# Where GpSimd's splits stand between VectorE's combinations, and which operand VectorE's spread sums read

## The reference, cut to what matters

```python
# group A: 4 heads, differential; two softmaxes per head, one subtracted from the other
p = probs(qb1, k1) - lam * probs(qb2, k2)
ao = einsum('bhqk,bkhd->bqhd', p, v)          # then rmsnorm per head, times silu(ag)
# group B: 8 heads of width 64; each row attends to its 256 best keys by an indexer score
s  = einsum('bqhd,bqkhd->bhqk', qb, kg) * scale + bias
bo = einsum('bhqk,bqkhd->bqhd', softmax(s), vg)   # times silu(bg)
y  = rmsnorm(x + einsum('bse,ed->bsd', concatenate([ao, bo]), w_out))
```

## Time and profile before

| | |
|---|---|
| median of three runs | 738.67 us |
| profiled execution | 737.92 us |
| span of the profile | 736.1 us |
| TensorE busy | 714.5 us (97%) |
| VectorE busy | 615.0 us (84%) |
| GpSimd busy | 363.1 us (49%) |
| ScalarE busy | 321.6 us (44%) |

### The profile page before, as it was taken

The page is one execution under the profiler, slowest core; times in us unless marked ns, Lnnn a source line. Parts: engine busy times, 40 slices in busy tenths (PEclk is TensorE's granted clock), DMA queues, the critical chain, the costliest instruction groups (busy, mean ns, idle before and its releaser), DMA issues.

```text
span 736.1 us, 12004 instructions
## 1 busy us (share of the span) xinstructions
PE 714.5 (97%) x4112; PEld 592.7 (81%) x4112; DVE 615.0 (84%) x1351; ACT 321.6 (44%) x723; POOL 363.1 (49%) x445
## 2 busy tenths in 40 slices
PE   8999999999999899999999999999999999999996
PEld 7757888888888788888888888888787878788886
DVE  5578999999998889888699999999789888546554
ACT  7547131131313666666631131314877767522222
POOL 5220222223556769771135654546999999612210
PEclk9999999999999999999999999999999999999999
DMA  7351211211220010213021112130010122313231
GB/s 282 108 145 46 52 49 44 57 44 46 66 76 1 0 44 1 51 31 101 16 71 45 43 44 57 44 87 0 30 45 11 50 55 91 116 58 100 73 115 57
DMA packets 25140, 45.10 MB, mean 61 GB/s; under 512 B 3140, under 2 KB 11512, under 8 KB 24952
## 3 DMA queue, kind: packets, MB, share of 16 engines
q1 hardware_dynamic: 23912, 43.28, 20.2%
q10 hardware_dynamic: 1168, 1.05, 0.4%
HBM read 35.92 MB, written 6.57 MB: 58 GB/s over the span
## 4 chain that ended last, share of the span: by engine, by line
PE 51%; DVE 23%; POOL 18%; issue 4%; ACT 2%; DMA 2%; POOLq 0%; SPq 0%; ACTq 0%; DVEq 0%
PE psum L1288 24%; PE psum L1509 12%; DVE score L1655 10%; DVE top L1650 10%; POOL k_high_twice L628 3%; PE psum L1383 2%; PE psum L1371 2%; PE psum L1208 2%; PE psum L1180 2%; POOL qT_r L631 2%; POOL k_zero_low L631 2%; POOL q_low_high L631 2%; POOL kT_r L631 2%; POOL near_low L769 2%; PE psum L1349 2%
## 5 line engine op out<-in xcount | busy, mean ns | idle before, releaser
L624 POOL TENSOR_TENSOR w_lo<-w_raw,w_hi 128x512 fp32r<-128x512 f32 x60 | 77.5, 1294 | 214.7 <-ACT w_hi L822 214.4
L1655 DVE MATCH_REPLACE8 score<-top,score 128x640 f32<-128x640 f32 (+5 forms) x176 | 157.4, 908 | 0.0
L1650 DVE MAX8 top<-score 128x8 f32<-128x640 f32 (+5 forms) x176 | 148.7, 911 | 1.2
L822 ACT ACTIVATE w_hi<-w_raw 128x512 fp32r<-128x512 f32 x60 | 37.4, 629 | 209.8 <-PE psum L1288 206.8
L998 ACT ACTIVATE probs<-psum,small 128x384 f32<-128x384 f32 (+7 forms) x128 | 94.6, 740 | 39.5 <-DVE small L1748 38.0
L1288 PE MATMUL psum<-big_hi,w_hi 128*128 128x512 f32 x256 | 99.7, 389 | 0.0
L1288 PE MATMUL psum<-big_hi,w_lo 128*128 128x512 f32 x256 | 99.6, 389 | 0.0
L1288 PE MATMUL psum<-big_lo,w_hi 128*128 128x512 f32 x256 | 99.6, 389 | 0.0
L1288 PE MATMUL psum<-w_hi,big_hi 128*128 128x512 f32 x192 | 74.7, 389 | 0.0
L1288 PE MATMUL psum<-w_lo,big_hi 128*128 128x512 f32 x192 | 74.7, 389 | 0.0
L1288 PE MATMUL psum<-w_hi,big_lo 128*128 128x512 f32 x192 | 74.7, 389 | 0.0
(11 more groups left out here) (199 smaller groups left out, 1608.8 us busy)
## 6 DMA issues: line engine op xcount, KB each, us to landing
w_raw<-in_w_in SPq DMA_DIRECT2D x62, 256.0 KB, 2.7
xs<-in_x SPq DMA_DIRECT2D x8, 512.0 KB, 6.5
k_high_twice<-k_high_twice SPq DMA_DIRECT2D x16, 256.0 KB, 3.7
xres<-in_x SPq DMA_DIRECT2D x8, 512.0 KB, 4.8
out_y<-y_out SPq DMA_DIRECT2D x8, 384.0 KB, 2.9
w_tail<-in_w_out SPq DMA_DIRECT2D x10, 256.0 KB, 2.6
bias_scratch<-bias_row SPq DMA_DIRECT2D x1, 2304.0 KB
bias<-bias_scratch SPq DMA_DIRECT2D x12, 128.0 KB, 3.1
```

The lines of the kernel that those rows point to most:

```text
L624: pool.tensor_tensor(lo[:, 0:cols], w_staged(n)[:, 0:cols], hi[:, 0:cols].bitcast(f32), ALU.subtract).then_inc(w_lo_made, 1)
L822: act.activation(w_parts(n)[0][:, 0:cols], w_staged(n)[:, 0:cols], ACT.Copy).then_inc(w_hi_made, 1)
L1650: ins = dve.max(top8[:, i - SEL0, :], sc)
L1655: ins = dve.match_replace(sc, top8[:, i - SEL0, :], sc, TAKEN)
```

## The change

In the first attention a quarter split is cut in two (`steps`): part 0 has the first three instructions, part 1 the last two with the signal. Each part has a step of its own, and waits, beside the gate of its step, for `combined` to reach s + 3, which is the combination of step s + 2. Block 1's quarters 2 and 3 go to the steps 0 to 3, block 2's four quarters to the steps 4 to 11, block 3's to the steps 12 to 19. In the second attention `share` becomes a product of a constant tile of ones, which lies in PSUM in the second 128 columns of `BACK_BANK`, with the two inverted sums; a memset before the loop fills the ones.

```diff
-            def split_k(ph, b, half):
+            def split_k(ph, b, half, steps=(0, 1)):
...
-                link(rounded(k0[0:HEAD, c], kT[0:HEAD, b, c]))
-                link(rounded(k1[HEAD:P, c], kT[HEAD:P, b, c]))
-                link(rest(k1_low[b % 2][HEAD:P, c], kT[HEAD:P, b, c], k1[HEAD:P, c]))
-                link(rest(kT_r[0:HEAD, b, c], kT[0:HEAD, b, c], k0[0:HEAD, c]))
-                ins = pool.memset(kT_r[HEAD:P, b, c].bitcast(f32), 0.0)
-                if half == 1:
-                    ins.then_inc(kh_made, 1)
...
+                if 0 in steps:
+                    link(rounded(k0[0:HEAD, c], kT[0:HEAD, b, c]))
+                    link(rounded(k1[HEAD:P, c], kT[HEAD:P, b, c]))
+                    link(rest(k1_low[b % 2][HEAD:P, c], kT[HEAD:P, b, c], k1[HEAD:P, c]))
+                if 1 in steps:
+                    link(rest(kT_r[0:HEAD, b, c], kT[0:HEAD, b, c], k0[0:HEAD, c]))
+                    ins = pool.memset(kT_r[HEAD:P, b, c].bitcast(f32), 0.0)
+                    if half == 1:
+                        ins.then_inc(kh_made, 1)
...
-                ahead = s + 3
-                if s < 2 or ahead >= TILES and ahead % TILES < 4 and ahead < 3 * TILES:
+                ahead = s + 4
+                if s < 4 or ahead >= TILES and ahead < 3 * TILES:
                     pool.wait_ge(o_gated, s + 1)
-                if s < 2:
-                    split_part(0, 1, s + 2)
-                elif ahead >= TILES and ahead % TILES < 4 and ahead < 3 * TILES:
-                    split_part(0, ahead // TILES + 1, ahead % TILES)
+                    pool.wait_ge(combined, s + 3)
+                if s < 4:
+                    split_part(0, 1, 2 + s // 2, (s % 2,))
+                elif ahead >= TILES and ahead < 3 * TILES:
+                    split_part(0, ahead // TILES + 1, ahead % TILES // 2, (ahead % 2,))
...
+            ones = bank(BACK_BANK)[:, P:2 * P]
...
-                dve.tensor_copy(shares[:, :, :], rinv[:, c:c + 2].unsqueeze(2).broadcast_to([P, 2, HEAD])
-                                ).then_inc(shares_made, 1)
+                dve.tensor_tensor(shares[:, :, :], ones.rearrange("p (m d) -> p m d", m=2),
+                                  rinv[:, c:c + 2].unsqueeze(2).broadcast_to([P, 2, HEAD]), ALU.mult
+                                  ).then_inc(shares_made, 1)
...
             dve.wait_ge(bank_moved, moved[9])
+            link(dve.memset(ones, 1.0))
```

More of the change, by code:

```diff
@@ L631, in rest, with split_q @@
                 return pool.tensor_tensor(out, src, high.bitcast(f32), ALU.subtract)
-            def split_q(ph, b, half):
+            def split_q(ph, b, half, steps=(0, 1)):
                 c = slice(half * HALF, (half + 1) * HALF)
@@ L649, in split_k @@
-            def split_k(ph, b, half):
+                if 0 in steps:
+                    link(rounded(q1[HEAD:P, c], qT[HEAD:P, b, c]))
+                    link(rest(q1[0:HEAD, c], qT[HEAD:P, b, c], q1[HEAD:P, c]))
+                    link(rounded(part, qT[0:HEAD, b, c]))
+                if 1 in steps:
+                    link(rest(qT_r[HEAD:P, b, c], qT[0:HEAD, b, c], part))
+                    ins = rounded(qT_r[0:HEAD, b, c], qT[0:HEAD, b, c])
+                    if half == 1:
+                        ins.then_inc(split, 1)
+                        pool.wait_ge(split, ph * BLOCKS + b + 1)
+                    else:
+                        link(ins)
@@ L658, in split_k @@
-                if half == 1:
-                    ins.then_inc(kh_made, 1)
[L660 to L664, removed]
+                if 0 in steps:
+                    link(rounded(k0[0:HEAD, c], kT[0:HEAD, b, c]))
+                    link(rounded(k1[HEAD:P, c], kT[HEAD:P, b, c]))
+                    link(rest(k1_low[b % 2][HEAD:P, c], kT[HEAD:P, b, c], k1[HEAD:P, c]))
+                if 1 in steps:
+                    link(rest(kT_r[0:HEAD, b, c], kT[0:HEAD, b, c], k0[0:HEAD, c]))
+                    ins = pool.memset(kT_r[HEAD:P, b, c].bitcast(f32), 0.0)
+                    if half == 1:
+                        ins.then_inc(kh_made, 1)
+                        pool.wait_ge(kh_made, ph * BLOCKS + b + 1)
+                    else:
+                        link(ins)
@@ L666, in split_part @@
+            def split_part(ph, b, j, steps=(0, 1)):
                 if j == 0 and b == 1:
                     wait_chunk_used(pool, (A_GROUPS, B_GROUPS)[ph][-1] * DB + DB - 1)
-                elif j == 0:
+                elif j == 0 and 0 in steps:
                     pool.wait_ge(s_ready, units_before(ph, b - 1))
-                (split_q, split_q, split_k, split_k)[j](ph, b, j % 2)
+                (split_q, split_q, split_k, split_k)[j](ph, b, j % 2, steps)
             def project_low(ph):
```

## The result

The changed kernel took 752.25 us in the median of four runs, against 738.32 us for four runs of the kernel before: the ratio is 1.0179, with a 95% interval of 1.0159 to 1.0200. The direction was as forecast, but the loss is 13.9 us instead of 4.6. The profiled execution has a span of 751.3 us, 15.2 more than before.

A forecast was written before the change was run, and what follows sets the result against it. The prediction took TensorE, busy 97% of the span, to bound the kernel. Added waits of 9.7 us less gains of 4.8 and 0.3 us made it 4.6 us slower, 743.3 us, range 740.2 to 747.0.

The forecast's parts named there:

- TensorE waits for the key copies at three block ends: First attention, starts of blocks 1 to 3: later key copies make TensorE wait 2.8, 4.1 and 2.8 us.
- The second wait is the longest, because of the low part in step 10: Block 2's start: the low part awaits ScalarE's high part, delaying the key's last difference; TensorE waits 4.1 us.
- What the first attention gains: First attention, splits moved behind combinations: less GpSimd contention with VectorE saves 4.8 us, bounds 3.0 and 6.1 us.
- Most of the contention goes: First attention: split parts fit the gaps between combinations; block 1's eight combinations fall from 9.9 to 7.5 us or less.
- The shares: Second attention: shares take 0.28 to 0.3 us each; only the last block gains, 0.3 us, bounds nothing and 0.9.
- The sum of the added waits as their price: First attention: three added TensorE waits cost their summed length, 9.7 us, bounds 8.6 and 11.5 us.
- every new wait of TensorE is paid in full: Whole kernel: TensorE is busy 97% of the span, so each added wait lengthens the time by its own length.
- The keys were not in time: Rival, block ends: copy and memset fit into TensorE's remaining work, only gains stay, 733.6 us; chance 0.07.
- gains and waits did not cancel: Rival, whole kernel: full gains of 6.1 and 0.9 us offset the waits, 738.8 us; chance 0.12.
- the pile-up after a wait: First attention, after each wait: VectorE and ScalarE start the next block with nothing behind them, giving back 0.5 us each.
- GpSimd did not fall behind: Rival, first attention: GpSimd's lateness piles up, gain 2 us, waits 12.7 us, time 749.1 us; chance 0.16.
- The forecast of a slower kernel: Whole kernel: the change makes it slower, by 4.6 us in the main forecast; chance of slower 0.78.

The follow-up runs named there:

- the kernel with early copies: Changed kernel with key copies signalled by the second rounding they read, not the later difference and memset: 734.43 us, ratio 0.9932 to the kernel before.
- its first part alone: Changed kernel with shares made by the copy again, only the first attention's splits changed: 751.23 us, ratio 1.0166 to the kernel before.
- the long waits: Kernel before, only the first attention's key copies for blocks 1 to 3 held until the combination of the block's seventh step: 756.93 us, ratio 1.0251.

## Why the prediction was wrong, step by step

- **TensorE waits for the key copies at three block ends: right.** Forecast 2.8, 4.1 and 2.8 us, 9.7 in all; measured 3.13, 4.10 and 3.33 us, 10.6 in all. The path was the forecast one: difference, memset, two issues, a copy of 3.96 us (3.86 us in the second case), 0.25 us to the start. The two shorter ones were a little longer because the combination of the sixth step, 1.03 to 1.05 us instead of 0.75, now met the gate: from its start to TensorE's asking it was 4.6 us, as in block 3 of before, so 3.6 us of slack were left behind its end instead of 3.9. At block 3 the second issue also came 0.4 us later. Redone from the prediction's own terms the bounds of this sum are 8.7 and 11.6 us rather than 8.6 and 11.5; nothing hangs on it.
- **The second wait is the longest, because of the low part in step 10: right, but not by the way that was forecast.** The low part was to wait for ScalarE's high part. That part was ready at 301.4, 0.6 us before GpSimd came to it; what held the low part was GpSimd's own order, the split behind its combination. The low part took 1.28 us instead of 1.77, the gate 0.88 instead of 0.45, and the combination that the last part waits for was stretched to 1.85 us, so that the part started only 0.4 us after it. The stretched combination alone made it some 0.8 us later, the rest of that queue 0.3 us more. That the size came out at 4.1 us is in part luck.
- **What the first attention gains: right in kind, too large.** 4.8 us were forecast, 3.8 us came: 0.5, 1.8 and 1.4 us in blocks 0, 1 and 2. But 1.6 us of these went when the waits went, as the kernel with early copies shows; rearranging the splits gave 2.1 us, less than the lower bound of 3.0. "Most of the contention goes" did not hold: block 1's combinations fell to 7.93 us, not to 7.5, and all 32 from 35.7 to 31.0 where 26.8 would be none. In block 2 `low(Q0 + 3)` stands behind a part 0, no longer fits the gap and meets a combination (1.99 us for one of 640 columns; 1.14 before, 0.88 in block 3); I had put nothing on that chunk. That this is what block 2 lacks is not shown: with the low parts moved that combination took 1.18 us, and block 2's first six steps still 25.98 us, as in the kernel with halves and early copies (25.97).
- **The shares: right.** 0.29 us each, and the gain ended in the fourth block's wait, which grew from 0.94 to 2.33 us. The forecast 0.3 us for the last block did not come in the trace. The first attention's gain and this one together are 1.3 us short of the forecast.
- **The sum of the added waits as their price: wrong.** This is the step that failed: "every new wait of TensorE is paid in full" took the idle time alone. After each wait TensorE worked at a granted clock of 0.50 for 3.4 to 5.9 us. That cost 7.5 us in all, which no term of the sum held and no bound allowed for. It is most of the 9.7 us between the forecast 4.6 and the 14.3 us of the traces; the waits are 0.9 us of it, the first attention's gain 1.0 and the shares 0.3. With the waits filled the low clock went and 6.3 us with it; with waits of the same length and nothing else changed it came, and after waits of 0.4 to 1.35 us it did not. The trace of before gave no row for it: TensorE's longest wait there is 1.67 us, and the clock stayed at 1.00 behind it. The range should have carried the unknown cost of waits longer than any that the trace shows. With the measured 7.5 us its upper end would have been 754.5 instead of 747.0 us, but no row of before gives that number.
- **The rivals.** The keys were not in time, and gains and waits did not cancel. What that rival said of the pile-up after a wait did happen: it gave back 0.5 us in block 1 and 1.1 us in block 2. GpSimd did not fall behind: three of the four parts 1 for block 2 started within 0.15 us of the combination that they wait for, the last, behind `wf_lo` and the gate, 0.4 us after it. The time of that rival (749.1 us) was nearer only by accident. The forecast of a slower kernel came true with a sum that lacked its second-largest term.

## What to carry to other kernels

A wait put on TensorE, where TensorE sets the time, can cost more than its length: here waits of 3.1 to 4.2 us cost 1.5 to 1.7 times their sum. Look for the granted clock behind it, and fill it if it can't be removed. When work is moved later, follow its signal through queue and copy to the consumer, and ask what the copy really reads: a signal placed one instruction group too late here decided between 1.8% slower and 0.7% faster. A gain ahead of a fixed arrival can show only when the arrival moves too. And what a stage gains beside new waits is not its gain without them (3.8 and 2.1 us here).

## What the runs showed of the hardware

- Behind all nine waits of 3.1 to 4.2 us (the changed kernel, its first part alone, the long waits) the granted clock was at 0.50, for 3.4 us in six cases and 6.8 us in three, the end of the wait included. Behind waits of 0.4 to 1.35 us it read 1.00. Between them it went both ways: 1.67 or 1.68 us, low in 4 of 14 traces; 1.82 us, low; 2.33 us, not.
- When it fell differed: at the first and third wait of the changed kernel about 1 us before TensorE started again (0.85 over the 3.2 us of the first), at the second and in the kernel with the long waits only after the start (1.00 through the wait, then 0.73 and 0.81).
- Transposes of an identity, whose output nobody reads, were enough to hold the clock at 1.00 through 3 to 4 us.
- A VectorE product with one input in PSUM and a broadcast of two SBUF numbers took 291 to 292 ns in 32 of 32 cases beside a busy GpSimd, where the copy from SBUF took 226 to 1341 ns.
